# Order of three steps inside the mixers' loop: maxima, copies of probabilities, keys

## The reference, cut to what matters

```
# mixer 1: sliding window attention, 8 heads of 64, blocks of 128 tokens, keys of this and the previous block
logits = scores - slopes * dist ; logits = where(valid, logits, -inf)
mx = maximum(logits.max(axis=-1), sink)
e = exp(logits - mx)
p = e / (e.sum(axis=-1) + exp(sink - mx))
out = einsum('bkgnqs,bnskd->bnqkgd', p, vv)        # then rms_norm over all heads
# mixer 2: mLSTM, 4 heads of 128, a state (c, n) carried from chunk to chunk
s = einsum('bhtd,bhsd->bhts', q, k) * exp(log_d - m_t)
num = s @ v + a_inter * (q @ c_st) ; den = s.sum(-1) + a_inter * (q . n_st)
h = num / maximum(abs(den), exp(-m_t))
c_new = decay * c_st + (k * w).T @ v
# memory: kv = rms_norm(mem) @ w_ckv
```

## Time and profile before

| | |
|---|---|
| Median of three runs | 2866.03 us (2861.99 to 2866.71) |
| Profiled execution | 2861.21 us, span 2859.5 us |
| TensorE busy | 2677.1 us, 94% of the span |
| VectorE busy | 1927.9 us, 67% |
| ScalarE busy | 1276.8 us, 45% |
| The mixers' stage | about 1750 to 1936 us of the span |

### The profile page before, as it was taken

The page is one execution under the profiler, slowest core; times in us unless marked ns, Lnnn a source line. Parts: engine busy times, 40 slices in busy tenths (PEclk is TensorE's granted clock), DMA queues, the critical chain, the costliest instruction groups (busy, mean ns, idle before and its releaser), DMA issues. The chain is left out here.

```text
span 2859.5 us, 38444 instructions
## 1 busy us (share of the span) xinstructions
PE 2677.1 (94%) x14346; PEld 2315.4 (81%) x14346; DVE 1927.9 (67%) x2433; ACT 1276.8 (45%) x1952; POOL 711.8 (25%) x446
## 2 busy tenths in 40 slices
PE   8989999999879999999989998889998999999993
PEld 7989999899768888878867887667785688888882
DVE  5366655463488777777984623765355899999996
ACT  4242332332333323334444214654332577777773
POOL 3000000002156555503610000005400144444441
PEclk9999999999989999999999998999998999999997
DMA  5342223343212222265632211114203799999996
GB/s 188 104 132 98 92 96 100 118 143 124 92 52 74 75 81 89 74 229 193 238 129 59 52 45 67 38 45 139 67 25 136 255 421 417 416 415 414 415 414 242
DMA packets 267201, 472.04 MB, mean 165 GB/s; under 512 B 24338, under 2 KB 183330, under 8 KB 241970
## 3 DMA queue, kind: packets, MB, share of 16 engines
q1 hardware_dynamic: 257554, 435.49, 42.2%
q0 software_dynamic: 9504, 34.61, 3.0%
HBM read 398.61 MB, written 71.43 MB: 164 GB/s over the span
## 5 line engine op out<-in xcount | busy, mean ns | idle before, releaser
L4072 DVE TENSOR_TENSOR k_w_lo<-k_raw,k_w_hi 128x2048 fp32r<-128x2048 f32 x192 | 433.4, 2287 | 34.7 <-ACT k_w_hi L4008 31.0
L4008 ACT CAST k_w_hi<-k_raw 128x2048 fp32r<-128x2048 f32 x192 | 363.1, 1912 | 64.2 <-PE bank L3926 41.2
L120 PE MATMUL bank<-u_hi,p_w_hi 128*128 128x342 f32 (+2 forms) x720 | 236.8, 329 | 8.9 <-DVEq L889 6.0
L121 PE MATMUL bank<-u_lo,p_w_hi 128*128 128x342 f32 (+2 forms) x720 | 231.1, 321 | 0.0
L122 PE MATMUL bank<-u_hi,p_w_lo 128*128 128x342 f32 (+2 forms) x720 | 230.8, 321 | 0.0
L3924 PE MATMUL bank<-k_w_hi,k_x_hi 128*128 128x512 f32 x512 | 203.1, 397 | 1.3 <-DVE k_x_lo L4078 1.0
L3926 PE MATMUL bank<-k_w_hi,k_x_lo 128*128 128x512 f32 x512 | 199.8, 390 | 0.0
L3925 PE MATMUL bank<-k_w_lo,k_x_hi 128*128 128x512 f32 x512 | 199.3, 389 | 0.0
L1467 PE MATMUL bank<-u_ffn_hi,f_w_hi 128*128 128x512 f32 (+3 forms) x520 | 170.4, 328 | 16.9 <-DVE f_inner L1757 8.4
L1468 PE MATMUL bank<-u_ffn_lo,f_w_hi 128*128 128x512 f32 (+3 forms) x520 | 167.0, 321 | 0.0
L1469 PE MATMUL bank<-u_ffn_hi,f_w_lo 128*128 128x512 f32 (+3 forms) x520 | 166.7, 320 | 0.0
(11 more groups left out here) (619 smaller groups left out, 7518.6 us busy)
## 6 DMA issues: line engine op xcount, KB each, us to landing
k_raw<-in_w_e_gate_dram SPq DMA_DIRECT2D x64, 1024.0 KB, 7.0
k_raw<-in_w_e_up_dram SPq DMA_DIRECT2D x64, 1024.0 KB, 7.6
k_raw<-in_w_e_down_dram SPq DMA_DIRECT2D x64, 1024.0 KB, 8.2
f_raw<-in_ffn_w_down_dram SPq DMA_DIRECT2D x77, 256.0 KB, 2.9
p_w<-in_w_in_dram SPq DMA_DIRECT2D x34, 512.0 KB, 4.2
f_raw<-inner_scratch SPq DMA_DIRECT2D x55, 256.0 KB, 3.3
f_raw<-in_ffn_w_gate_dram SPq DMA_DIRECT2D x22, 512.0 KB, 3.6
f_raw<-in_ffn_w_up_dram SPq DMA_DIRECT2D x22, 512.0 KB, 5.2
```

The costliest lines, as they stand in the source:

```text
L120: pe.matmul(out, wh[:, t, :], xh[t][:, c:c + n], start=t == 0, stop=False)
L121: pe.matmul(out, wh[:, t, :], xl[t][:, c:c + n], start=False, stop=False)
L4008: act.copy(wh[:, q, :], raw[:, r, :]).then_inc(hi_made, 1)
L4072: dve.tensor_tensor(wl[:, q, :], raw[:, r, :], wh[:, q, :], ALU.subtract).then_inc(lo_made, 1)
```

## The change

Three calls change their place in two of the four lists. On VectorE, `maxima(i + 1, 1)` goes from directly behind `logits(i + 1, (2, 3))` to directly behind `place(i - 1)`, so that `keep(i)` follows the logits (in block 0 the third part of the memory's copies stands between). On ScalarE, `keys(i + 1)` goes ahead of `exponentials(i + 1, 1)`. TensorE, GpSimd and the DMA queues keep their lists.

```diff
@@ -2935,7 +2935,6 @@
                 update(i)
                 if i < LAST:
                     logits(i + 1, (2, 3))
-                    maxima(i + 1, 1)
                 if i == 0:
                     memory_keep(2)
                 keep(i)
@@ -2944,6 +2943,8 @@
                 finish(i)
                 if i:
                     place(i - 1)
+                if i < LAST:
+                    maxima(i + 1, 1)
                 scale(i)
                 if i == 0:
                     memory_keep(3)
@@ -3043,9 +3044,9 @@
                 if i:
                     att_root(i - 1)
                 if i < LAST:
+                    keys(i + 1)
+                if i < LAST:
                     exponentials(i + 1, 1)
-                if i < LAST:
-                    keys(i + 1)
                 keep_inverse(i)
```

## The result

The changed kernel took 2846.62 us (median of four runs, 2843.45 to 2847.72), the kernel before 2865.63 beside it: ratio 0.9934, 95% interval 0.9918 to 0.9950, so 14 to 24 us less. The forecast was 2855.0, with a range from 2848 to 2862: right way, and 1.4 us outside the range. The mean of its 14 runs is 2849.6. That of all 62 runs of the kernel before is 2864.1 (34 of them belong to a comparison without the changed kernel): 14.5 us less. By the means of each comparison the gain is 18.9, 14.4 and 12.9 us, so the first lies highest. e5 ran on chip 15 and e7 on chip 10, the first comparison's chip is not on record; whether its extra is scatter or its chip can't be told.

The account below looks back on a forecast made before the run. TensorE bounds the program, but waits and low clock bound the mixers. Gain 12.45 at full clock less 1.44 for one low stretch, 11.0 us: 2850.2 from the profiled 2861.21, 2855.0 from the median 2866.03; range 2848 to 2862.

Parts of the forecast that it names:

- Copies sooner: VectorE's copies of transposed probabilities start 0.64 us behind the turning, 1.53 sooner; TensorE's wait falls from 1.88 to 0.35.
- K0: The moment VectorE begins to copy block 0's transposed probabilities in the mixers; 1778.20 us in the kernel before.
- The new last wait: In the mixers' loop, late exponentials delay ScalarE's copy of the inverse by 1.86 us at full clock; turns take 19.13.
- K: The moment VectorE begins to copy a block's transposed probabilities in the mixers' loop; times in a turn count from it.
- The last turn: The mixers' turn from K6 = 1904.38: its read comes at K + 10.1 instead of K6 + 9.65, losing 0.45 us.
- The full-clock sum: Mixers' gain at full clock throughout: 11.30 us from six turns, plus 1.60 in block 0, minus 0.45: 12.45.
- The clock: TensorE's granted clock in the mixers, the unknown: gain bounded by 12.45 us at full clock and 8.92 with low stretches unchanged.
- one low stretch: One stretch of low TensorE clock assumed left in the mixers, costing 1.44 us: 12.45 becomes 11.0 gained.
- The slower rival: Low clock moves behind new idle time ahead of TensorE's scores, 2.87 us per turn: 7.6 slower, 2873.7; chance 0.04.
- Behind the stage: After the mixers everything starts from their end, no earlier load still under way, so the gain reaches the end whole.
- The range: Whole kernel, 2848 to 2862 us: 12.5 gained and a median 5 lower, or 8.9 gained and the same spread.

Follow-up runs that it names:

- e5: The changed kernel again, no edit, with more rounds: 2851.58 us, ratio 0.9955 to the kernel before.
- e7: The changed kernel a third time, no edit: 2851.58 us, ratio 0.9961 to the kernel before.
- e6: The changed kernel with ScalarE's copy of the inverse moved ahead of the second exponentials: 2838.72 us, ratio 0.9904 to the kernel before.
- e4: The kernel before with twelve useless transposes in TensorE's 1.88 us gap, nothing moved: 2854.73 us, ratio 0.9964.
- e9: The kernel before with five useless transposes in TensorE's 1.88 us gap: 2858.10 us, ratio 0.9981.
- e2: The changed kernel with ScalarE's exponentials put back ahead of the keys, so only the VectorE part: 2861.45 us, ratio 0.9994 to the kernel before.
- e3: The kernel before with only the ScalarE part, keys ahead of the second exponentials: 2865.16 us, ratio 1.0008.
- e8: The kernel before, no edit, profiled a third time: one run, 2864.93 us.

## Why the prediction was right and wrong

- *Copies sooner.* Predicted 0.64 behind the turning, idle 0.35: measured 0.63 and 0.35. Block 0 gave 1.56 us (K0 less the stage's begin, 27.20 to 25.64) for 1.60.
- *The new last wait.* Predicted ScalarE's copy at K + 8.08, read at K + 10.1, turns of 19.23 and five of 19.13: measured 8.07, 10.06, and 19.28 with five of 19.09 to 19.10. TensorE's idle time ahead of the scores was put at 1.1 and is 0.98. The last turn lost 0.41 for 0.45.
- *The full-clock sum.* 12.45 us, measured 12.6 to 12.9 for the stage over three profiles of either kernel. e6 shows the cause of the 1.4 us per turn that the change leaves: the exponentials in front of the copy.
- *The clock.* That the gap behind the first turning brings the low clock is shown by e4, where filling it alone gives clock 1.00 in every turn from K1. The chosen value was wrong by a little: I kept one low stretch, 1.44 us, and took 11.0; there was none. The page's rule of short idle times that keep the clock swinging (the Trainium skill, "TensorE: Matmul & The Clock Gate", section "A second HAM failure mode: psum-queue depth-cycling") did not hold for the changed kernel, whose turns keep 1.00 with idle times of 0.35, 0.79, 0.98 and 0.24, the first even with 1.44 and the last with 2.36. The clock did swing in e9, before and e2, with single idle times of 1.33, 1.88 and 2.06. No length of one idle time parts the two groups. The slower rival did not come, but e2 shows its mechanism at work, with 2.06 us idle ahead of the transposes that the scores follow.
- *The step that failed* is "Behind the stage": that the gain reaches the end whole, with nothing added there, a term put at nothing. Behind the mixers the changed kernel is 2.6 to 3.1 us shorter (301.6 to 298.5, 299.0, 298.6), by the clock in the router's stage. With the stage's 12.6 that makes 15.2 to 15.7, less perhaps 0.6 given back behind the experts' first matmul, against 14.5 by the means of all runs. The low stretch that was kept and did not come adds its 1.44 to the miss: the forecast gain of 11.0 was too small by these two terms, 4 us in all.
- *The range* was too narrow below, and bad luck had a part: 11.0 and the two terms give some 2851, inside it, and the two later medians (2851.58 both) lie inside it too. Its lower end was 12.5 gained and a median run 5 lower than the three shown, so 2848. That left out those 3 us, and it took the scatter from three runs (4.7 us); 34 runs of the kernel before spread over 15 us (2855.95 to 2870.83), and medians of four move with them. The first comparison's 19.0 is 4.5 above the mean over all comparisons.

What stays open: why the router's stage has the better clock in the changed kernel. e3, whose mixers are as slow as before, has it too (299.0); e4, whose mixers are shorter, has not (301.7); e6 and e9 lie between (300.3, 300.2). e2, with mixers as slow as before, has it as well (299.1). It does not follow the length of the mixers' stage. Both programs that were profiled three times gave the same value each time, and every profile near 299 is of a program that holds the change or a half of it; but whether it follows the program or chance can't be told from three profiles each, and what sets the clock behind the same idle time of 2.30 us is not shown. Of the 10 us by which the begin of the mixers varies, a part is there early: TensorE's first matmul of L792 starts at 234.67 us in the first profile of the kernel before, 1.1 us earlier in e5, 3.3 later in e8. What causes it is not shown.

## What to carry to other kernels

When an engine waits in a ring, move what others don't wait for behind what they do, and then go through each queue behind the moved work: the late exponentials stood in front of the one copy that the ring needed, and one more swap took another 9.0 us from the stage, after the 12.6 of the first change. Read the granted clock turn by turn before pricing a wait on TensorE: where the clock fell behind an idle time of 1.9 us, the turn took 1.6 to 2.9 us more than the turn with the same idle time at full clock. Take the scatter of a kernel from tens of runs, not from three, when one per cent of its time decides.

## What the hardware showed that was not expected

- Filling 1.47 us of a 1.88 us gap with useless transposes made the kernel 10.4 us faster (e4), with the gap's idle time down to 0.57 us and the clock at 1.00 in all turns from K1.
- Which turns fall to the low clock is repeated exactly from run to run: three profiles of the kernel before agree in every turn to 0.1 us, although the stage begins up to 4.5 us apart.
- The same work behind the same idle time can run at either clock in two programs, each of them repeatable: behind 2.30 us idle in the router's stage it took 16.5 us in two profiles of the kernel before and 14.93 in two of the changed kernel.
